# GpSimd scales a head's attention map by one two-input product, and TensorE waits for each rotated query tile where it first uses it

## The reference

```
def _softmax(s, sink):
    if sink is None:
        return jax.nn.softmax(s, axis=-1)
    m = jnp.maximum(jnp.max(s, axis=-1, keepdims=True), sink)
    p = jnp.exp(s - m)
    return p / (jnp.sum(p, axis=-1, keepdims=True) + jnp.exp(sink - m))
...
        qa = _rms(qa.reshape(b, n, HEADS_A, d), qn_a)
        ka = _rms(ka.reshape(b, n, KV_A, d), kn_a)
...
        if use_rope:
            qa, ka, qb, kb = _rope(qa, cos, sin), _rope(ka, cos, sin), _rope(qb, cos, sin), _rope(kb, cos, sin)
...
    oa_x = _window_attend(qa_x, ka_x, va_x, ka_c, va_c, sink)
    ob_x = _dense_attend(qb_x, jnp.concatenate([kb_c, kb_x], axis=1),
                         jnp.concatenate([vb_c, vb_x], axis=1), None)
```

## Time and profile before

| | us |
|---|---|
| median of 3 executions | 2136.09 (2135.9 to 2137.53) |
| the profiled execution's own time | 2135.81 |
| its span in the profile | 2134.4 |
| TensorE busy | 2010.7 (94% of the span) |
| VectorE busy | 1395.5 (65%) |
| ScalarE busy | 1029.9 (48%) |
| GpSimd busy | 463.3 (22%), of which L715 78.8 |

### The profile page before, as it was taken

The page is one execution under the profiler, slowest core; times in us unless marked ns, Lnnn a source line. Parts: engine busy times, 40 slices in busy tenths (PEclk is TensorE's granted clock), DMA queues, the critical chain, the costliest instruction groups (busy, mean ns, idle before and its releaser), DMA issues.

```text
span 2134.4 us, 32820 instructions
## 1 busy us (share of the span) xinstructions
PE 2010.7 (94%) x12924; PEld 1689.8 (79%) x12924; DVE 1395.5 (65%) x2355; ACT 1029.9 (48%) x1916; POOL 463.3 (22%) x356
## 2 busy tenths in 40 slices
PE   6999999999999899999999789999999999989999
PEld 4776677888987776899976457788898776769999
DVE  4393657867978666655564654786797866566555
ACT  3444644432543646654554553444254365555443
POOL 1000316412531003100100671642253100000000
PEclk9999999999999999999999999999999999999999
DMA  9641521548349635456535003144832721114564
GB/s 339 215 156 60 178 80 60 183 130 274 138 160 283 202 99 180 149 170 214 153 125 180 38 2 99 52 178 135 267 100 87 255 88 60 60 52 149 171 204 117
DMA packets 276745, 311.65 MB, mean 146 GB/s; under 512 B 6128, under 2 KB 260208, under 8 KB 269424
## 3 DMA queue, kind: packets, MB, share of 16 engines
q1 hardware_dynamic: 271888, 304.90, 43.8%
q10 hardware_dynamic: 4704, 4.65, 0.7%
HBM read 308.48 MB, written 1.05 MB: 145 GB/s over the span
## 4 chain that ended last, share of the span: by engine, by line
PE 68%; DVE 15%; ACT 8%; issue 3%; POOL 3%; DMA 2%; ACTq 0%; SPq 0%; DVEq 0%; POOLq 0%
PE bank L778 67%; DVE weights_low L1523 3%; DVE weights_low L1904 2%; ACT weights_high L2312 1%; DVE scratch L1515 1%; DVE yT L1515 1%; ACT big L2755 1%; DVE input_low L1515 1%; PE bank L787 1%; DVE big L2049 1%; DMA parameter_columns<-p_columns 1%; DVE big L1515 1%; DMA modulation_slots<-p_modulation_rows 1%; DVE modulation_slots L1549 1%; DVE hidden_low L1918 1%
## 5 line engine op out<-in xcount | busy, mean ns | idle before, releaser
L778 PE MATMUL bank<-input_high,weights_high 128*128 128x256 f32 (+1 forms) x2336 | 750.2, 323 | 27.6 <-DVE scratch L1942 10.3
L778 PE MATMUL bank<-input_high,weights_low 128*128 128x256 f32 (+1 forms) x2336 | 736.5, 317 | 0.0
L778 PE MATMUL bank<-input_low,weights_high 128*128 128x256 f32 (+1 forms) x2336 | 715.1, 317 | 5.2 <-DVE input_low L1515 5.2
L1523 DVE TENSOR_TENSOR weights_low<-weight_slots,weights_high 128x1024 fp32r<-128x1024 f32 (+2 forms) x344 | 387.1, 1164 | 188.0 <-ACT weights_high L2312 187.7
L778 PEld LDWEIGHTS bank<-input_high,weights_high 128*128 128x128 f32 x2336 | 440.7, 189 | 87.0 <-issue 28.9
L778 PEld LDWEIGHTS bank<-input_low,weights_high 128*128 128x128 f32 x2336 | 434.6, 189 | 43.3 <-DVE input_low L1515 10.0
L778 PEld LDWEIGHTS bank<-input_high,weights_low 128*128 128x128 f32 x2336 | 440.3, 188 | 33.4
L2312 ACT ACTIVATE weights_high<-weight_slots 128x1024 fp32r<-128x1024 f32 (+2 forms) x348 | 314.6, 951 | 150.2 <-PE bank L778 137.0
L1904 DVE TENSOR_TENSOR weights_low<-weight_slots,weights_high 128x512 fp32r<-128x512 f32 x216 | 233.4, 1100 | 35.8 <-ACT weights_high L2590 33.9
L778 PE MATMUL bank<-hidden_high,weights_high 128*128 128x256 f32 (+1 forms) x704 | 238.5, 339 | 0.6 <-DVE weights_low L1523 0.4
L778 PE MATMUL bank<-hidden_high,weights_low 128*128 128x256 f32 (+1 forms) x704 | 237.6, 338 | 0.0
(11 more groups left out here) (277 smaller groups left out, 2804.6 us busy)
## 6 DMA issues: line engine op xcount, KB each, us to landing
weight_slots<-w_gu SPq DMA_DIRECT2D x44, 1024.0 KB, 5.2
weight_slots<-ffn_w_in SPq DMA_DIRECT2D x44, 1024.0 KB, 5.2
modulation_slots<-p_modulation_rows SPq DMA_DIRECT2D x64, 512.0 KB, 4.7
modulation_slots<-mod_w SPq DMA_DIRECT2D x32, 1024.0 KB, 6.5
modulation_slots<-w_mod SPq DMA_DIRECT2D x28, 1024.0 KB, 6.8
weight_slots<-w_in SPq DMA_DIRECT2D x24, 1024.0 KB, 8.4
weight_slots<-w_down SPq DMA_DIRECT2D x16, 768.0 KB, 4.9
weight_slots<-ffn_w_out SPq DMA_DIRECT2D x16, 768.0 KB, 4.9
```

Source lines behind the costliest of these rows:

```text
L778: return pe.matmul(o, w, r, start=start, stop=stop, skip_group_check=shared)
L1523: tt(m.w_low[:, g % 2, c], m.ring[:, g % SLOTS, c], m.w_high[:, g % 2, c].bitcast(F32), ALU.subtract).then_inc(m.low_made.sem, 1)
```

## The change

It has two parts. In `even_weights` GpSimd's tensor_scalar by a per-partition scalar becomes a tensor_tensor product, whose second input is the reciprocal spread over the row by a stride of zero. For kinds 0 and 1 the count stays at one operation for each head. For kind 2 two operations of 128x256 become one of 128x512. In `even_mixer` the wait for all rotations is dropped. The scores of units 3, 6, 9, ... wait for the rotation of their own query tile. Ahead of the first turns there is a wait for the first operation of rotation 9, the one that reads bank 7.

```
             for half in range(2):
-                for c in range(1 if kind < 2 else 2):
-                    t = slice(0, TOK) if kind < 2 else (X, C)[c]
-                    x = m.PT[:, n % 3, half, t]
-                    i = pool.tensor_scalar(x, x, m.ev_rec[:, n % 3, half, c:c + 1], None, ALU.mult)
+                x, r = m.PT[:, n % 3, half, :], m.ev_rec[:, n % 3, half, :]
+                if kind < 2:
+                    i = pool.tensor_tensor(x, x, r[:, 0:1].to_broadcast([P, TOK]), ALU.mult)
+                else:
+                    i = pool.tensor_tensor(x.rearrange("p (c q) -> p c q", c=2), x.rearrange("p (c q) -> p c q", c=2),
+                                           r.unsqueeze(2).to_broadcast([P, 2, SEQ]), ALU.mult)
                 i.then_inc(m.even_weighted.sem, 1)
...
         pe.wait_ge(*m.keys_spread.end(L))
-        pe.wait_ge(*m.rotated.end(L))
         for n in range(UNITS + 1):
             if n + AHEAD < UNITS:
+                if n % 3 == 0:
+                    pe.wait_ge(*m.rotated.at(L, 3 * (2 + (n + AHEAD) // 3) + 2))
                 even_scores(n + AHEAD)
+            if n == 0:
+                pe.wait_ge(*m.rotated.at(L, 3 * (len(EVEN_NORMED) - 1)))
             if n < UNITS:
                 even_flip(n)
```

## The result

| | before | changed |
|---|---|---|
| median of 5 executions, one chip, us | 2136.09 (2133.34 to 2139.11) | 2149.1 (2145.35 to 2153.35) |
| span of the profiled execution | 2134.4 | 2147.6 |

The ratio is 1.0057, with a 95% interval of 1.0042 to 1.0073: the changed kernel is slower by 13 us. The forecast of 2134.5 and its range up to 2138.4 are missed. It went the way of rival B, which had 9%, and twice as far.

What follows compares the result with a forecast made beforehand. VectorE and ScalarE by turns were taken to bound the attention loop, with GpSimd only in the chain's end. Terms -0.58, +0.97, -1.05, -0.93 gave -1.59 us, a forecast of 2134.5 us, range 2131.8 to 2138.4.

Steps and rivals of the forecast that it cites:

- rival B: Part 0's shifts: a product under 1.21 us lets the second in, shifts wait for it; +6.3 us in all, 9%.
- term 2: Shifts of part 0: eight of nine cost nothing, unit 7's falls into the second product; +0.97 us.
- Term 1: Loop start: unit 3's scores no longer wait for rotation 9, so its maxima start earlier despite held rotations; -0.58 us.
- Term 3: Part 1: four 128x4 shifts wait less for GpSimd's first operation, 0.20 instead of 0.46 us, others stay; -1.05 us.
- Term 4: End of the loop: the last unit's two products finish earlier, so the last turns and product follow earlier; -0.93 us.
- Rival A: Start and shifts: VectorE is not held by a product with a spread input; 2132.3 to 2132.7 us, 13%.
- C: GpSimd's product is dear, 1.62 us, so part 0's shifts wait longer; +2.0 us together, 2138.1 us, 8%.

Runs made afterwards that it cites:

- e4: Changed kernel, but GpSimd's second product of each unit waits until VectorE's shift of the next unit is done: 2134.38 us, ratio 0.9986 to the kernel before.
- e9: Changed kernel with the map multiplied by a row of another tile instead of the spread reciprocal: 2140.17 us, ratio 1.0006 to the kernel before.
- e1: Changed kernel with the old tensor_scalar put back, so only the new rotation waits remain: 2135.74 us, ratio 0.9992 to the kernel before.
- e5: Changed kernel with the map multiplied by itself instead of by the spread reciprocal: 2150.91 us, ratio 1.0061 to the kernel before.
- e6: Changed kernel with the sum of map and spread reciprocal instead of their product: 2151.71 us, ratio 1.0058 to the kernel before.
- e8: e4 with one more wait: unit 1's first product also waits for the last rotation; 2132.38 us, ratio 0.9969 to the kernel before.
- e2: Kernel before with only the new product, old rotation waits kept: 2150.39 us, ratio 1.0053 to the kernel before.
- e10: Old tensor_scalar with the new rotation waits, its second operation waiting for the next unit's shift: 2136.61 us, ratio 0.9995 to the kernel before.
- e7: Changed kernel with each head's product cut into two of 128x256, four per unit: 2142.87 us, ratio 1.0016 to the kernel before.
- e3: Changed kernel with each unit's second map scaled by the old tensor_scalar, the first by the product: 2139.12 us, ratio 1.0009 to the kernel before.

## Why the prediction was wrong

**The step that failed** is the length of the product, "I take 1.30", with the bound "1.21 below". I read it from six rows of one kind of operation, a sum of two different full rows, and took them for every two-input operation. It was 1.04, outside both bounds. The prediction says that "the trace has no product with a spread input", and so nothing in it could carry a bound from below. The bound of 1.21 was only the value at which the sign turns.

**The mechanism of rival B was right, its point was not.** It said that a first product which is over by 1.21 lets the second one in, and the shift pays for all of it. That is what the rows show, and e4, which takes only this meeting away, gives 17.2 us back, 14.7 of it in parts 0 and 1. But "it decides at 1.21" was too low. The second operation begins before the first one's end, and with 1.27 five of the eight shifts that I had as free are held (e9; part 0 +6.04, where term 2 says +0.97). The prediction's words "0.09 to run, less than the 0.14 that are hidden: no cost" are true only for a shift that comes ahead of the second operation's start. That distance decides, and with 1.30 it would have been a few hundredths (an estimate: the second starts 0.04 before the first one's end in e9, the shifts come at 1.21 to 1.23). That alone should have given rival B much more than 9%. The kernel lost twice what B says because B was priced at 1.20 and had a gain of 1.15 in part 1; at 1.04 part 1 loses 6.69.

**Term 1** (-0.58) measured -1.14, by the short product: the two rotations are held 1.16 and 1.15 instead of the 1.4 each that I had. With 1.27 (e9) it measured -0.68, and with the old operation beside it -1.46 (e1), as worked out. This step was sound and took the wrong length. TensorE's gap of 3.31 is 0.60 in the changed kernel, and its granted clock from 1184 to 1186 is 1.00, where it was 0.50.

**Term 2** (+0.97) measured +6.10. Eight shifts lose some 0.66 each and unit 7's loses 0.38: 5.7. Unit 12's, which this part of the table takes in, loses another 0.65. That makes 6.3, so 0.2 of it lies beside other work.

**Term 3** (-1.05) measured +6.69 in part 1. It rested on the length too. These shifts come 1.14 to 1.16 behind GpSimd's start, ahead of the end of a product of 1.30 and behind that of one of 1.04. So "the other shifts of part 1 stay" fell with the length, and all of them are held: 4 x (0.65 + 0.74 + 0.46) = 7.4 for the three kinds, less the 0.65 of unit 12 gives 6.7, and 6.69 is measured. With 1.27 (e9) none is held and part 1 gains 1.48, so near its own length the term was right in its sign and 0.4 short. Where no shift is held (e4) part 1 gains 1.51: the 1.16 of the four 128x4 shifts from 0.46 to 0.17, and 0.1 for each of three 128x2 ones.
That a shift with one SBUF input can be held stood in the earlier trace rows. The Trainium skill has this too, and the prediction cites only the half on two inputs: SBUF — State Buffer, Who interferes with whom, names tensor_scalar among the VectorE operations that can take the port pair shared with GpSimd, and VectorE: DVE Perf Modes, Mode 2×_2P, says that this needs a single source and its destination both in SBUF with fitting dimensions, in float32 too. The runs agree as to the holding: 0.92 beside GpSimd's product, 0.17 without it.

**Term 4** (-0.93) measured +1.65 in the changed kernel and -0.90 in e4, e5, e6 and e8. My "nothing that would swallow it" holds there. The gap by itself is not the loss: e5 has the same one, of 2.42, and its product follows at full speed (timeline of e5):

```profile
1281.38 0.92 DVE L2063 TENSOR_SCALAR big<-big 128x4 f32<-128x4 f32 x1
...
1283.04 0.63 PE L788 MATMUL bank<-ident,big 128*128 128x128 f32 x4 [2.42 <-DVE yT L2082]
1283.60 1.08 PE L779 MATMUL bank<-yT,scratch 128*64 128x256 f32 x8
```

The changed kernel's product took 1.98 there (rows above), and so did e1's, at 1270.41, behind a gap of 1.67. So the lower clock is the difference, 8.22 against 5.67 or 2.55 of the 13.30 in the profiled executions. The same gap brought it in one execution and not in another: a gap of 2.42 in e2 (0.50) and e6 (1.00), one of 1.67 in e1 and e10 (0.50) and in e4, e8 and the kernel before (1.00). What decides that I can't say. The medians don't show the 2.55: e5 and e6 are no quicker than the changed kernel (1.0061 and 1.0058 against 1.0057).

**Rival A and the rule on rates.** VectorE is held, so A is out. C had the length the other way. The Trainium skill (GPSIMD Engine Reference, Engine selection) puts two-input work behind one-input work; here the two-input product is the quicker, 1.04 against 1.57, and even with two different rows 1.27.

**What stays open.** Why a tensor_scalar holds VectorE only for its first 0.70 us; I have the two lengths and no cause. It also doesn't fit the 128x4 shifts of the earlier trace rows, which arrive 1.12 behind a tensor_scalar's start and still wait to its end, while the two-input shifts of part 0 at 1.21 are free. And why TensorE's clock fell at the end in some executions.

## What to carry to other kernels

Where two engines hold each other, the sum of busy times says little; what counts is which operation of the one is running at the moment at which the other arrives. Making an operation shorter can put the next one under that moment, so work out the arrival against each operation's start, and give a near miss the chance of a hit. Where such a meeting is certain to fall near the edge, one wait that lets the short operation of the ring (the chain that sets the loop's time) go first costs little (e10 against e1: 0.12 us) and makes the shorter operation worth having (e4 and e8, 3.9 us).
A duration from "the nearest row" is a bound only if that row has the same inputs: one tile or two, a full row or a spread one.

## What I had not expected of the hardware

- GpSimd's tensor_tensor of 128x512 took 1.04 us with one full row as input (by itself, or with one number for each partition) and 1.27 with two different ones (e9); in 128x256 it took 0.61 (e7) against 0.92 for the tensor_scalar.
- GpSimd's tensor_scalar, which looked harmless, holds a small VectorE operation that comes in its first 0.70 us (128x512) or 0.49 us (128x256), as in e3, with one exception there (0.17 at 0.01 behind the start).
- Of two GpSimd products without a wait between them the second begins some 0.04 us before the first one's end. A VectorE operation that came 0.001 to 0.004 us behind that start waited for all of it, and one that came 0.001 to 0.011 ahead of it did not wait (e9).
- The same gap on TensorE, 2.41 or 2.42 us, went with a granted clock of 0.50 from 1278.5 to 1285.2 in the changed kernel and with 1.00 in e5: 2.55 us of difference at the end.
